# One loop of 28 units for the query, key and value projections, with the residual update and two norms in pieces inside it

## The reference, cut to what matters

```python
h = h + g2 * rms_norm(f, norm_g[i, 3])            # end of layer 0: f is the ConvFFN's output
a = rms_norm(h, norm_g[i, 0]) * (1.0 + sc1) + sh1 # start of layer 1, latent tokens; the same for context
q, k, v = jnp.split(h @ w_qkv, [q_dim, q_dim + kv_dim], axis=-1)   # here h is a: (1024, 1024) @ (1024, 1536)
q, k = apply_axial_rope(q), apply_axial_rope(k)                    # latent tokens
kc, vc = jnp.split(hc @ w_qkv[:, q_dim:], 2, axis=-1)              # 256 context tokens, keys and values only
```

## Time and profile before

| what | value |
| --- | --- |
| median of three runs | 3034.64 us |
| profiled execution, its own time | 3032.49 us |
| span of its trace | 3030.7 us |
| PE busy | 2747.4 us (91%) |
| DVE busy | 2064.8 us (68%) |
| ACT busy | 1280.9 us (42%) |
| mean granted TensorE clock | 0.954 of full speed |

### The profile page before, as it was taken

The page is one execution under the profiler, slowest core; times in us unless marked ns, Lnnn a source line. Parts: engine busy times, 40 slices in busy tenths (PEclk is TensorE's granted clock), DMA queues, the critical chain, the costliest instruction groups (busy, mean ns, idle before and its releaser), DMA issues. The chain is left out here.

```text
span 3030.7 us, 44962 instructions
## 1 busy us (share of the span) xinstructions
PE 2747.4 (91%) x17388; PEld 2473.3 (82%) x17388; DVE 2064.8 (68%) x2883; ACT 1280.9 (42%) x1888; POOL 132.4 (4%) x177
## 2 busy tenths in 40 slices
PE   5898888999999989999988498999899999999996
PEld 3888776999998989999976366777889999878785
DVE  3899988888975565655745547666478457584665
ACT  4231244433445353333431527777554334443332
POOL 0000000000000000000000002333000000000000
PEclk7999988999999999999998798999999999999998
DMA  6444422222221212222221120000122322233332
GB/s 261 152 160 146 149 102 89 79 84 92 90 77 65 81 56 89 79 87 94 71 89 56 42 76 9 1 1 1 56 84 85 97 97 88 94 95 120 97 97 83
DMA packets 66519, 263.14 MB, mean 87 GB/s; under 512 B 6960, under 2 KB 7216, under 8 KB 60080
## 3 DMA queue, kind: packets, MB, share of 16 engines
q1 hardware_dynamic: 58368, 213.17, 21.4%
q0 software_dynamic: 5760, 41.95, 3.9%
q10 hardware_dynamic: 2224, 5.69, 0.5%
HBM read 256.58 MB, written 4.19 MB: 86 GB/s over the span
## 5 line engine op out<-in xcount | busy, mean ns | idle before, releaser
L1603 PE MATMUL PS<-a_hi,w_hi 128*128 128x322 f32 (+7 forms) x3584 | 922.8, 326 | 113.5 <-DVE w_lo L962 58.4
L1603 PE MATMUL PS<-a_lo,w_hi 128*128 128x322 f32 (+7 forms) x3584 | 905.4, 321 | 0.0
L1603 PE MATMUL PS<-a_hi,w_lo 128*128 128x322 f32 (+7 forms) x3584 | 904.0, 321 | 0.0
L1603 PEld LDWEIGHTS PS<-a_hi,w_hi 128*128 128x128 f32 x3584 | 617.8, 194 | 168.7 <-DVE w_lo L962 73.2
L1603 PEld LDWEIGHTS PS<-a_lo,w_hi 128*128 128x128 f32 x3584 | 620.5, 194 | 25.2 <-issue 2.1
L1603 PEld LDWEIGHTS PS<-a_hi,w_lo 128*128 128x128 f32 x3584 | 617.1, 193 | 25.3
L962 DVE TENSOR_TENSOR w_lo<-raw,w_hi 128x1024 fp32r<-128x1024 f32 (+2 forms) x380 | 443.3, 1171 | 224.1 <-ACT w_hi L481 217.5
L481 ACT ACTIVATE w_hi<-raw 128x1024 fp32r<-128x1024 f32 (+2 forms) x380 | 385.7, 1015 | 1.6 <-DVE zB L1474 1.4
L1603 PE MATMUL PS<-z_hi,w_hi 128*128 128x320 f32 (+1 forms) x1056 | 301.3, 340 | 30.4 <-DVE z_lo L1351 28.3
L1603 PE MATMUL PS<-z_lo,w_hi 128*128 128x320 f32 (+1 forms) x1056 | 299.2, 338 | 0.0
L1603 PE MATMUL PS<-z_hi,w_lo 128*128 128x320 f32 (+1 forms) x1056 | 299.0, 338 | 0.0
(11 more groups left out here) (242 smaller groups left out, 3126.0 us busy)
## 6 DMA issues: line engine op xcount, KB each, us to landing
raw<-wstream SPq DMA_DIRECT2D x380, 512.0 KB, 3.5
ada_slot<-adastream POOLq DMA_DIRECT2D x40, 1024.0 KB, 5.2
ada_first<-adastream SPq DMA_DIRECT2D x4, 2048.0 KB, 19.8
h<-xT SPq DMA_DIRECT2D x1, 2640.0 KB, 14.6
h<-xT ACTq DMA_DIRECT2D x1, 2480.0 KB, 9.9
out<-h ACTq DMA_DIRECT2D x1, 2048.0 KB, 9.3
out<-h SPq DMA_DIRECT2D x4, 512.0 KB, 2.7
rope_sb<-rope ACTq DMA_DIRECT2D x1, 1024.0 KB, 4.9
```

The costliest lines, as they stand in the source:

```text
L1603: last = MM(PS[:, 2 * j + m, 0:n], wt[:, j, k, :], mv[:, k, m * n:(m + 1) * n], start=(k == 0 and p_ == 0), stop=(k == tiles - 1 and p_ == 2))
```

## The change

The three phases and the two norms between them become one phase of 14 pairs, in the order A1, B1, C1 (12, 12 and 4 units). Its loop runs over single units t instead of pairs. In step t PE does unit t and then the rotation or turn of unit t - 1. DVE does `rope_last` of unit t - 2 (L1513 and L1516 of before), `rope_first` of unit t - 1 (L1510), the weight split of unit t + 1, then a piece of other work, then `key_low`. ACT does the weight split of unit t + 1, a piece of other work, the key or value copies of unit t - 2, then the copy of unit t.

The residual update of tokens 640 to 1279 (`post0`) begins in the ConvFFN before: as each of its last output tiles is added, ACT squares it and DVE adds it to a running sum (the path `last=`, which another ConvFFN of the kernel already has); a root of a constant (`root_warm`) goes ahead of the first real root. Two sums, the last square, the mean, the root, the reciprocal, the scaling and the updates are pieces of steps 0 to 6, the context's updates of steps 13 and 14. The norm of B1 (`pre1`) is made tile by tile in steps 3 to 10 and its high and low parts at the change from unit 11 to unit 12. That of C1 lies in steps 14 to 22, its high and low parts at the change from unit 23 to 24. The sums go by seven additions of one tile each instead of three of four, two and one. Tiles B1 and C1 get buffers of their own (`qh[1]`, `o_low`). Later phases only get other semaphore counts.

The diff, cut to its core (removed bodies, waits for buffers and the renumbered counts left out):

```diff
-    post_b = dict(kind="post", layer=0, which=1, chunk=B, y="zB", t="zA", hosted=True, after_ffn=True)
+    post_b0 = dict(kind="post0", chunk=B, y="zB", sq=40, sums=35, updates=16, hosted=True)
+    pre_b1 = dict(kind="pre1", chunk=B1, sq=48, sums=42, hosted=True)
+    pre_c1 = dict(kind="pre1", chunk=C1, sq=56, sums=49, hosted=True)
...
-          dict(kind="ffn", layer=0, chunk=B, w=HALF, pairs=n0, y="zB", units=[("ffn0", 0, n0)], head=post_a, tail=pre_a1, begun=True),
-          pre_a1, post_b,
-          dict(kind="qkv", chunk=A1, pairs=6, order=[2, 3, 4, 5, 0, 1], head=post_b)]
-    for c, n in ((C1, 2), (B1, 6)):
-        ph += [dict(kind="pre", layer=1, which=0, chunk=c, w=c["n"], t="o32"),
-               dict(kind="qkv", chunk=c, pairs=n, order=list(range(n)))]
+          dict(kind="ffn", layer=0, chunk=B, w=HALF, pairs=n0, y="zB", units=[("ffn0", 0, n0)], head=post_a, tail=pre_a1, last=post_b0,
+               begun=True),
+          pre_a1, post_b0, pre_b1, pre_c1,
+          dict(kind="qkv", pairs=14, parts=[(A1, [2, 3, 4, 5, 0, 1]), (B1, [0, 1, 2, 3, 4, 5]), (C1, [0, 1])],
+               post=post_b0, pres=[pre_a1, pre_b1, pre_c1])]
...
                 act.wait_ge(norm_step, x["s"] + 9)
                 act.dma_start(out[:, :, t0:t0 + w], h[:, :, t0:t0 + w]).then_inc(stored, 16)
+
+            def pre1_square(x, k, updates):
+
+                t0, w = x["chunk"]["t0"], x["chunk"]["n"]
+                act.wait_ge(h_updated, updates + k + 1)
...
+                    def key_or_value_out(u, at_unit):
+
+                        j, t0, w, g = at_unit % 2, u["t0"], u["w"], 2 * u["tile"]
+                        if u["kind"] == "k":
...
+                            act.wait_ge(v_turned, u["v"] + 1)
+                            A(v_sb[:, t0 // BLK:(t0 + w) // BLK, u["tile"] * P:(u["tile"] + 1) * P],
+                              PS[:, 6 + j, 0:w].rearrange("p (a b) -> p a b", b=P), ACT.Copy).then_inc(v_stored, 1)
+
+                    for t in range(30):
+                        q, j = q0 + t // 2, t % 2
+                        if t < 28 and t not in (12, 24):
                             split(q + j, 1 - j)
...
+                        if t == 0:
+                            act.wait_ge(y_added, x["d"])
+                            act.dma_start(rope_sb[:], rope).then_inc(rope_loaded, 16)
+                            y_square(post, 7)
+                            root(post["s"] + 1, HALF, 6)
+                        if t in (3, 4, 5):
+                            for k in range((0, 2, 6)[t - 3], (2, 6, KT)[t - 3]):
+                                pre1_square(pre_b1, k, post["updates"])
+                        if t == 7:
+                            root(pre_b1["s"] + 1, 512, 6)
+                        if t in (9, 10):
+                            for m in range(2 * (t - 9), 2 * (t - 8)):
+                                modulate(pre_b1["n"], m, pre1_tiles(pre_b1, m), 1, 0, 512)
+                        if t in (14, 15):
+                            act.wait_ge(in_lo, 4 * pre_b1["n"] + 4)
+                            for k in range(4 * (t - 14), 4 * (t - 13)):
+                                pre1_square(pre_c1, k, post["updates"] + 8)
+                        if t == 18:
+                            root(pre_c1["s"] + 1, CTX, 6)
+                        if t in (21, 22):
+                            for m in range(2 * (t - 21), 2 * (t - 20)):
+                                modulate(pre_c1["n"], m, pre1_tiles(pre_c1, m), 1, 0, LAT)
+                        if t >= 2:
+                            key_or_value_out(x["list"][t - 2], t - 2)
+                        if t >= 28:
+                            continue
+                        u = x["list"][t]
...
+                        act.wait_ge(unit_done, 2 * q0 + t + 1)
+                        nxt = {11: pre_b1, 23: pre_c1}.get(t)
+                        if nxt:
+                            high_part(nxt["n"], 0, pre1_tiles(nxt, 0))
+                        A(rb[j][:, 0:u["w"]], slot(j, u["w"])[:, 0], ACT.Copy).then_inc(evacuated, 1)
+                        if nxt:
+                            high_part(nxt["n"], 1, pre1_tiles(nxt, 1))
+                            split(q + 1, 1)
+                            for m in (2, 3):
+                                high_part(nxt["n"], m, pre1_tiles(nxt, m))
...
+            def post0_scale(x, first, last_k):
+
+                y = wide[x["y"]]
+                dve.wait_ge(norm_step, x["s"] + 3)
+                TT(y[:, first:last_k, 0:LAT - HALF], y[:, first:last_k, 0:LAT - HALF],
+                   rms[:, 0:LAT - HALF].unsqueeze(1).to_broadcast([P, last_k - first, LAT - HALF]), ALU.mult).then_inc(norm_step, 1)
+
...
+            def post0_update(x, first, last_k):
+
+                for k in range(first, last_k):
+                    dve.wait_ge(norm_step, x["s"] + 4 + k // 4)
+                    hk = h[:, k, HALF:LAT]
+                    STT(hk, wide[x["y"]][:, k, 0:LAT - HALF], mod[0][:, 0, 40 + k:41 + k], hk, ALU.mult, ALU.add).then_inc(h_updated, 1)
...
+                    post, (pre_a1, pre_b1, pre_c1) = x["post"], x["pres"]
+
+                    def rope_first(at_unit):
+
+                        u, j = x["list"][at_unit], at_unit % 2
+                        if not u["roped"]:
+                            return
+                        t0, w = u["t0"], u["w"]
+                        keys = u["k"] - (at_unit > 0 and x["list"][at_unit - 1]["kind"] == "k")
...
+                        TT(tb[j][:, 0:w], rb[j][:, 0:w], rope_sb[:, 0, t0:t0 + w], ALU.mult).then_inc(rope_step, 1)
...
+                    def rope_last(at_unit):
+
+                        u, j = x["list"][at_unit], at_unit % 2
+                        if not u["roped"]:
+                            return
+                        t0, w, r3 = u["t0"], u["w"], 3 * u["r"]
+                        dve.wait_ge(rot_done, u["r"] + 1)
+                        dve.wait_ge(rope_step, r3 + 1)
+                        TT(rb[j][:, 0:w], PS[:, 4 + j, 0:w], rope_sb[:, 1, t0:t0 + w], ALU.mult).then_inc(rope_step, 1)
+                        dve.wait_ge(rope_step, r3 + 2)
+                        dst = tb[j][:, 0:w] if u["kind"] == "k" else qh[t0 // 512][:, u["tile"], 0:w]
+                        TT(dst, tb[j][:, 0:w], rb[j][:, 0:w], ALU.add).then_inc(rope_step, 1)
+
...
+                    cm_sum(post, 6)
+                    cm_sum(post, 7)
+                    dve.wait_ge(rope_loaded, 16)
+                    for t in range(30):
+                        q, j = q0 + t // 2, t % 2
+                        nxt = {12: pre_b1, 24: pre_c1}.get(t)
+                        if nxt:
+                            for m in range(4):
+                                remainder(nxt["n"], m, pre1_tiles(nxt, m))
+                                if m == 1:
+                                    split(q, 1)
+                        if t >= 2:
+                            rope_last(t - 2)
+                        if 1 <= t <= 28:
+                            rope_first(t - 1)
+                        if t < 28 and not nxt:
                             split(q + j, 1 - j)
...
+                        if t == 1:
+                            invert(post["s"] + 2, HALF)
+                            post0_scale(post, 0, 4)
+                        if t == 2:
+                            post0_scale(post, 4, 8)
+                            post0_update(post, 0, 2)
+                        if t == 3:
+                            post0_update(post, 2, 6)
+                        if t == 4:
+                            post0_update(post, 6, 8)
+                            pre1_sum(pre_b1, 1, 3)
+                        if t == 5:
+                            pre1_sum(pre_b1, 3, 6)
+                        if t == 6:
+                            pre1_sum(pre_b1, 6, 8)
+                            post0_scale_context(post)
+                        if t == 7:
+                            invert(pre_b1["s"] + 2, 512)
+                        if t in (8, 9):
+                            for m in range(2 * (t - 8), 2 * (t - 7)):
+                                pre1_normed(pre_b1, m)
+                        if t in (13, 14):
+                            post0_update_context(post, 4 * (t - 13), 4 * (t - 12))
+                        if t in (15, 16):
+                            pre1_sum(pre_c1, 1 if t == 15 else 4, 4 if t == 15 else 8)
+                        if t == 19:
+                            invert(pre_c1["s"] + 2, CTX)
+                        if t == 20:
+                            for m in range(4):
+                                pre1_normed(pre_c1, m)
+                        if t >= 2:
+                            key_low(t - 2)
...
+                    def c1_average():
+                        pe.wait_ge(v_stored, 4)
+                        average_summed(pre_c1["sums"] + 7, pre1_total(pre_c1), CTX, 6)
...
+                    def turned_or_rotated(at_unit):
...
```

(63 more changed lines are left out.)

158 lines of the change are left out of this document (66 added, 92 removed).

## The result

The changed kernel takes 2950.94 us (median of four runs, 2950.50 to 2953.52), the kernel before, run beside it, 3034.58 us (3032.40 to 3034.97). The ratio is 0.9726, 95% interval 0.9713 to 0.9738: 83.6 us faster. The profiled execution took 2953.52 us, its span is 2951.7 us.

The account below looks back on a forecast made before the run. Queue order and chunk changes bound the kernel. From first projection unit to first attention score, 169.7 us of TensorE's own work plus remaining waits give 186.1 instead of 263.4 us, so 3034.64 - 77.2 = 2957.4 us; range 2947 to 2978.

Parts of the forecast that it names:

- (1) to (5): TensorE's own work in the new stage: 24 units, 20 rotations, value turns, 4 context units, three means; 169.7 us.
- (6): Unit 0: waits for the third `a_lo` and for the residual's mean; 3.5 us lost, bounds 1 and 7.
- (7): Units 1 to 11: DVE's steps 1 to 9 take 57.5 of 58.4 us; 0.5 us taken, bounds 0 and 10.
- (8) to (10): Waits at A1 to B1 (2.8 us), B1 to C1 (2.8) and for C1's weights (0.7); bounds together 3 and 13.
- (11): Slow matmuls at lowered clock behind the waits left in the stage; 1 us, bounds 0 and 3 x 2.5.
- Rival C: Clock falls behind each of three remaining waits, 3 x 2.5 = 7.5 us, so 2964 us; chance 0.05.
- (12): Wait ahead of the first attention score, kept at 5.15 us; bounds 3 and 6.
- Rival A: DVE becomes the bound, with 98% load over steps 1 to 9: 2970 us; chance 0.13.
- Rival B: Chunk changes still stall as pieces of B1's and C1's norms come late: 24.5 us more, 2982; chance 0.06.
- Rival D: Handover one deep, DVE late for good: 10.1 us per unit, 3048 us, slower than before; chance 0.04.
- E: Saved waits only move to the ends of the stage and the time stays; chance 0.02.

Follow-up runs that it names:

- kernel with both edits: Against the changed kernel: residual's mean moved from unit 0 to unit 1, and first high parts written inside units 11 and 23; 2946.92 us.
- kernel with early high parts alone: Against the changed kernel: at both chunk changes the next chunk's first high parts written inside units 11 and 23, not behind them; 2949.90 us.

## Why the prediction was right

- **The bound** (order of the queues and chunk changes, not load): right. With its waits gone, the same work takes 182.7 us.
- **(1) to (5), PE's own work, 169.7:** rotations were 0.87, not 0.945: the rhythm is 6.405 us. 20 x 0.08 = 1.6 us less. In a pair the rotations began at 1796.66, while the copy of the second unit, which the second rotation needs, ended at 1797.51: the price read there probably held a wait; this was not tested. The three means took 0.94 (timeline), 0.88 and 0.46 (by how much longer their units took), 0.7 us less than the 3.0.
- **(6) Unit 0:** waits 0.77 and 1.83, 2.6 us where 3.5 were counted. That the unit ends 11.3 us after its start against 10.9 is in part luck: the mean was priced at 1.8 and took 0.94, and the three k steps behind it at 2.1 and took 3.9, most of them at half clock.
- **(7) Steps 1 to 11:** no wait for `w_lo`. The forecast 0.5 was a margin. The load of 98% was too dark: DVE is busy 56.7 of 64.3 us in units 1 to 10, and of the added work 4 to 7 us went free.
- **(8) to (10):** waits of 2.11 in unit 12, 0.73 and 1.11 in unit 24, none for the weights of C1: 4.0 us where 6.3 were counted. Unit 12 still ends 9.9 us behind unit 11 (forecast 9.2), as it holds slow matmuls.
- **(11) Clock, 1.0:** too low. Behind 1.83 us and behind 2.11 us of waiting the clock fell to 0.50 for some 3 us each; at the second seven matmuls took 0.43 us each: about 1.6 us each time. The reading behind the term failed: of the wait of 5.36 us only the first matmul behind it was looked at, and the ones behind it not. There the trace of the kernel before has 5.4 us at half clock:

```profile
1763.10:1768.50 5.40, 5.40 (x13) 4.24 (x14) 1.06 (x1) 0.00 (x0) 0.00 (x0) 0.51 0.55 194
```

- **Rival C** was thus right in kind for two waits of three, at two thirds of its price. The Trainium skill, "TensorE: Matmul & The Clock Gate", on HAM oscillation, says that repeated idle gaps put PE back to half clock; the trace agrees for these two waits, but not for unit 24's 0.73 and 1.11 us, behind which no fall came.
- **(12) Start of attention, 5.15:** 0.9 us too high. The 5.15 held the last unit's rope operations, which a context value unit doesn't have; the first score waits 2.72 us, but the last turn ahead of it now waits 1.49 for its copy.
- **Rival A** costs 14.4 us of stage only when 22 us of work are added. **Rival B**: the price of exposed norms, forecast 24.5 us for both, is 29.4; its sign, a wait for `a_lo` over 5 us, did not come (2.11). **Rival D** priced a DVE that stays late at 10.1 us per unit. The kernel with 22 us of work more comes nearest: its units 2 to 10 take 7.6 to 9.1 us each, and from unit 13 on it is back at the changed kernel's pace. **E** is excluded.

Stage: forecast 186.1, measured 182.8; time: 77.2 less forecast, 83.6 measured. The terms missed both ways: too much by 1.6, 0.7, 0.9, 0.5, 2.3 and 0.9, too little by 2.2 for the clock. That is 4.7 us less than forecast, where 3.3 were measured; 1.4 us were not taken apart. Of the 6.4 us by which the time is off, 3.3 are the stage's. The rest is no step of the forecast: the two profiled executions lay 2.1 us below and 2.6 us above their medians, which is 4.7, less 1.6 us by which the second was later outside the stage.

Where the 80.6 us come from: both norms inside the units 29.4; the residual's long pieces at most 23.7, by the kernel before without them (the changed kernel still does this work, in pieces); 10.6 us of waits at the two key pairs, read from the trace, not tested alone; 0.9 of waits at the start of attention. Some 16 us more lie in the rest (first pair, slow matmuls) and were not taken apart; the start of the residual in the ConvFFN before was not tested alone either. The late rotation is no such share: by pairs a unit took 6.49 us, so the order by units alone brings 0.08 us each. It is what keeps the new order from costing 23 us.

## What to carry to other kernels

Where an engine's queue holds both what TensorE needs next and long side work, put the former first and cut the latter to pieces shorter than the slack of a step; measure the slack by adding dummy work until the time moves. A norm with nothing beside it costs its whole chain (17 and 12 us here). Cut into pieces, the first of them went into steps 3 to 10 without a wait of PE, in a loop in which DVE was then busy 88% of the time (56.7 of 64.3 us), so there was not much room left. In an order by single units, give each dependent matmul one unit of distance.

## What the runs showed of the hardware

Waits of 1.7 to 2.1 us can bring the granted clock to 1.2 GHz for about 3 us, and not at once: behind the wait that ended at 1655.04 five matmuls ran at full pace, 1.2 us in all, before it fell. This costs nearly as much again as the wait (some 1.6 us). It is not certain: in the kernel with both edits waits of 2.0 us ahead of unit 1 and of 1.74 us in unit 24 left the clock at 1.00, while in the kernel with early high parts alone it fell behind the same 1.74 us. So the gain of an edit that shortens a wait can be lost by a fall elsewhere, as in that kernel. And of two executions of the same kernel the one with a clock of 0.91 where the other had 1.00, from 1050 to 1070 us, came to the stage 2.4 us later, as much as several of the edits tried here bring.
